# Feed-forward's first four outputs from the sum in front of its norm, with the norm's weights as two more columns

## What is computed

```python
x = layer_norm(alpha * x + mix, ln1_g[l], ln1_b[l])
ff = swiglu_ffn(x, w_ffn_gate[l], w_ffn_up[l], w_ffn_down[l])
x = layer_norm(alpha * x + ff, ln2_g[l], ln2_b[l])
...
def swiglu_ffn(x, w_gate, w_up, w_down):
    return (jax.nn.silu(x @ w_gate) * (x @ w_up)) @ w_down
```

## Time and profile before

| | |
|---|---|
| median of 3 runs | 893.04 us (893.03 to 893.29) |
| profiled execution | 894.56 us, its span 892.8 us |
| TensorE matmuls busy | 872.5 us (98%) |
| VectorE busy | 627.1 us (70%) |
| ScalarE busy | 440.3 us (49%) |
| granted TensorE clock, mean | 0.996 |

### The profile page before, as it was taken

How to read it: one execution, slowest core, us unless ns; L and a number is a source line. 1 busy time by engine, 2 the same in 40 slices (tenths; PEclk the granted TensorE clock), 3 DMA queues, 4 the chain that set the end, 5 groups by cost and what they waited for, 6 DMA issues and landing times.

```text
span 892.8 us, 13280 instructions
## 1 busy us (share of the span) xinstructions
PE 872.5 (98%) x5324; PEld 709.2 (79%) x5324; DVE 627.1 (70%) x1252; ACT 440.3 (49%) x750; POOL 21.2 (2%) x16
## 2 busy tenths in 40 slices
PE   8999999999999999999999999999999999999996
PEld 4678477776687777877998888988999888888885
DVE  5532757594836759966699999978688775665666
ACT  3351515543723356555544444566554665555552
POOL 0000000000000000000002121100000000000000
PEclk9999999999999999999999999999999999999999
DMA  9784551100354033203556656441366365546541
GB/s 351 284 319 171 203 197 61 48 25 1 119 196 161 16 130 142 84 23 142 167 189 188 190 173 204 142 143 59 103 196 210 113 201 206 188 175 204 190 164 47
DMA packets 39997, 136.68 MB, mean 153 GB/s; under 512 B 4352, under 2 KB 4480, under 8 KB 39680
## 3 DMA queue, kind: packets, MB, share of 16 engines
q1 hardware_dynamic: 38928, 130.48, 42.8%
q10 hardware_dynamic: 1008, 5.36, 1.6%
HBM read 134.77 MB, written 1.05 MB: 152 GB/s over the span
## 4 chain that ended last, share of the span: by engine, by line
PE 68%; DVE 25%; ACT 3%; DMA 2%; issue 1%; SPq 0%; DVEq 0%; ACTq 0%
PE ps L414 8%; DVE wlo L1472 7%; PE ps L971 6%; DVE AF L1941 6%; PE ps L415 4%; PE ps L369 4%; PE ps L370 4%; PE ps L374 3%; PE ps L733 3%; PE ps L489 3%; PE ps L386 2%; DMA AF<-wmod 2%; PE ps L397 2%; PE ps L756 2%; PE ps L398 2%; PE ps L401 2%
## 5 line engine op out<-in xcount | busy, mean ns | idle before, releaser
L1472 DVE TENSOR_TENSOR wlo<-raw,whi 128x1024 fp32r<-128x1024 f32 (+2 forms) x204 | 231.6, 1158 | 34.4 <-ACT whi L1009 34.2
L1009 ACT ACTIVATE whi<-raw 128x1024 fp32r<-128x1024 f32 (+2 forms) x204 | 203.5, 1005 | 86.2 <-DMA raw<-wpack 45.8
L369 PE MATMUL ps<-hx,whi 128*128 128x256 f32 (+1 forms) x384 | 115.4, 300 | 0.3 <-ACT AF L1350 0.3
L414 PE MATMUL ps<-hx,whi 128*128 128x512 f32 x320 | 113.9, 398 | 0.0
L370 PE MATMUL ps<-hx,whi 128*128 128x256 f32 (+1 forms) x384 | 112.0, 292 | 0.0
L374 PE MATMUL ps<-hx,wlo 128*128 128x256 f32 (+1 forms) x332 | 96.9, 292 | 0.0
L415 PE MATMUL ps<-hx,wlo 128*128 128x256 f32 x320 | 89.8, 281 | 0.0
L369 PEld LDWEIGHTS ps<-hx,whi 128*128 128x128 f32 x384 | 73.3, 191 | 3.8 <-issue 2.3
L370 PEld LDWEIGHTS ps<-hx,whi 128*128 128x128 f32 x384 | 73.4, 191 | 2.0 <-issue 0.7
L459 PE MATMUL ps<-whi,hx 128*128 128x512 f32 (+1 forms) x192 | 71.7, 373 | 0.2 <-ACT acc L1078 0.2
L414 PEld LDWEIGHTS ps<-hx,whi 128*128 128x128 f32 x320 | 60.1, 188 | 14.6
(11 more groups left out here) (293 smaller groups left out, 1667.2 us busy)
## 6 DMA issues: line engine op xcount, KB each, us to landing
raw<-wpack SPq DMA_DIRECT2D x178, 512.0 KB, 4.1
AF<-wmod SPq DMA_DIRECT2D x48, 512.0 KB, 6.0
raw<-wpack SPq DMA_DIRECT2D x24, 256.0 KB, 2.7
XT<-xin SPq DMA_DIRECT2D x4, 512.0 KB, 6.0
raw<-wpack SPq DMA_DIRECT2D x4, 432.0 KB, 4.9
uq<-wuq ACTq DMA_DIRECT2D x2, 768.0 KB, 5.4
cst<-cpack ACTq DMA_DIRECT2D x1, 1093.0 KB, 8.0
AF<-wukv ACTq DMA_DIRECT2D x2, 512.0 KB, 6.7
```

The costliest lines, as they stand in the source:

```text
L369: e.matmul(o, wh[:, b], xh(k), start=j == 0, stop=False, skip_group_check=True)
L414: e.matmul(ps.ap(key, 512).rearrange("p (s n) -> p s n", s=2), wh[:, b], K.hx[:, :, k, 0:256], start=k == 0, stop=False, skip_group_check= ...
L1009: e.activation(W.hi(i), W.raw(i), ACT.Copy).then_inc(*HI.up(j))
L1472: e.tensor_tensor(W.lo(i), W.raw(i), W.hi(i), ALU.subtract).then_inc(*LO.up(j))
```

## The change

Four things, all around the first norm of the second block.

1. fg0, up0, fg1 and up1 are made by a new function `lin_raw` from the sum in front of the norm, scaled by the norm's weight g. Rows of 258 columns are multiplied: 256 tokens, then two columns with the norm's weight and bias. So each output has, beside the product, the product of the weight with g and with b, from which mean, scale and bias are put in afterwards (`normed`, three instructions on DVE for each of the four outputs, with PSUM read by two of them, and a bias in the silu). The rows lie in the second half of `hx`, whose row grows from 512 to 528 columns. ACT makes the high half of each scaled tile (`raw_high`), DVE the low half (`raw_low`), tiles 0 to 4 during the `w_o` stage and 5 to 7 after the inverse root.
2. The sums and the two spreads of the norm are issued by PE between the first three k of `lin_raw`; the `keep` matmuls there go away. ACT copies m and r from PSUM to SBUF, and DVE reads them there.
3. The transposes and their copies move from f = 0 to 3 to f = 2 to 5. fg2 and up2 are put in the banks of s1 and s2, fg3 and up3 in those of m and r.
4. The conversions are placed anew: fg2 in front of the norm's tiles, up2's high half on ACT at tile 5 and its low half on DVE behind tile 7, fg3 at the start of f = 0, up3 at the start of f = 1.

```diff
+RAW = 2
...
@@ -403,9 +405,9 @@
         W.given[c] = M.now()
         ps.drop(key)
 
-    def lin_wide(key, wname, cols, xw):
-
-        free = ps.take(key)
+    def lin_wide(key, wname, cols, xw, at=None):
+
+        free = ps.take(key, at=at)
         c, wh, wl = weights(key, (wname, 0, tuple(range(KD)), cols), KD * P)
         pe.wait_ge(*free)
         for k in range(KD):
@@ -947,14 +949,34 @@
         pe.wait_ge(V["ln1", "dg", what], *ps.take(("ln1", what)))
         e.matmul(ps.ap(("ln1", what), 256), C("ones"), K.rs[:, z:z + 256], start=True, stop=True, skip_group_check=True).then_inc(*M.up(("ln1", what)))
 
-    keep(1)
-    ln1_sums("s1", K.acc[:, 0:256], K.XT[:, 7, XC], V["x1sum", 6], V["x1", 7])
-    ln1_sums("s2", K.acc[:, 256:512], K.sq[:, 768:1024], V["sqadd", 6], A["x1sq", 7])
-    ln1_spread("m", 256)
-    keep(2)
-    ln1_spread("r", 0)
-    keep(2)
+    rh, rl, rw = (lambda k: K.rx[:, 0, k, :]), (lambda k: K.rx[:, 1, k, :]), (lambda k: V["xr", k])
     xt3 = lambda k: V["x3", k]
+
+    def lin_raw(specs):
+
+        got = []
+        for key, wname, cols in specs:
+            free = ps.take(key)
+            got.append((weights(key, (wname, 0, tuple(range(KD)), cols), KD * P), free))
+        for k in range(KD):
+            b = slice(k * P, (k + 1) * P)
+            pe.wait_ge(A["gb"], A["xr", k], V["gb"], V["xr", k])
+            for (key, wname, cols), ((c, wh, wl), free) in zip(specs, got):
+                o = ps.ap(key, 258)
+                pe.wait_ge(*free)
+                e.matmul(o, wh[:, b], rh(k), start=k == 0, stop=False, skip_group_check=True)
+                e.matmul(o, wl[:, b], rh(k), start=False, stop=False, skip_group_check=True)
+                i = e.matmul(o, wh[:, b], rl(k), start=False, stop=k == KD - 1, skip_group_check=True)
+                if k == KD - 1:
+                    i.then_inc(*M.up(key))
+                    W.given[c] = M.now()
+            if k == 0:
+                ln1_sums("s1", K.acc[:, 0:256], K.XT[:, 7, XC], V["x1sum", 6], V["x1", 7])
+                ln1_sums("s2", K.acc[:, 256:512], K.sq[:, 768:1024], V["sqadd", 6], A["x1sq", 7])
+            if k == 1:
+                ln1_spread("m", 256)
+            if k == 2:
+                ln1_spread("r", 0)
 
     def down(f, ts):
 
@@ -977,12 +999,13 @@
     for f in range(KF):
         cc = (P * f, P)
         if f == 0:
-            lin_many([((nm, j), f"w_ffn_{w}_2", 0, (P * j, P), x2h, x2l, 256) for j in range(2) for nm, w in (("fg", "gate"), ("up", "up"))], lambda k: A["x3h", k], xt3)
-        elif f > 1:
-            lin_wide(("fg", f), "w_ffn_gate_2", cc, xt3)
-            lin_wide(("up", f), "w_ffn_up_2", cc, xt3)
-        if f < 4:
-            t, q = f // 2, f % 2
+            lin_raw([((nm, j), f"w_ffn_{w}_2", (P * j, P)) for j in range(2) for nm, w in (("fg", "gate"), ("up", "up"))])
+        elif f >= RAW:
+            at = [ps.bank.get(("ln1", x)) if f < RAW + 2 else None for x in (("s1", "s2") if f == RAW else ("m", "r"))]
+            lin_wide(("fg", f), "w_ffn_gate_2", cc, xt3, at[0])
+            lin_wide(("up", f), "w_ffn_up_2", cc, xt3, at[1])
+        if RAW <= f < RAW + 4:
+            t, q = (f - RAW) // 2, (f - RAW) % 2
             pe.wait_ge(A["x3", 4 * q + 3], *ps.take(("x3t", f)))
             for j in range(4):
                 i = e.transpose(ps.ap(("x3t", f), P, j * P), K.XT[:, 4 * q + j, 256 + t * P:384 + t * P], C("ident"))
@@ -1405,14 +1428,27 @@
             highs(("ao", m))
         ac.wait_ge(V["mgs", m], M["attn2"])
         e.activation(hh[:, m, 0:256], g.Gt[:, m, :], ACT.Copy, scale=0.5).then_inc(*A.up(("mg", m)))
+    def raw_high(m):
+        ac.wait_ge(V["x1", m])
+        e.activation(K.rx[:, 0, m, 0:256], XT[:, m, XC], ACT.Copy, scale=C("l1g", m, 1)).then_inc(*A.up(("xr", m)))
+
     highs(("wo", 0))
+    ac.wait_ge(K.c2["cst"], M["attn2"])
+    e.activation(K.rx[:, 0, :, 256:258], C("l1g", 0, 16).rearrange("p (s k) -> p k s", s=2), ACT.Copy).then_inc(*A.up("gb"))
     for m in range(KD):
         if m < 7:
             highs(("wo", m + 1))
+            raw_high(m)
         z = m % 4 * 256
         ac.wait_ge(V["x1", m], V["sqadd", m - 4] if m >= 5 else V["sqadd", 1] if m == 4 else None)
         e.activation(K.sq[:, z:z + 256], XT[:, m, XC], ACT.Square).then_inc(*A.up(("x1sq", m)))
+    raw_high(7)
     e.dma_start(K.AF[:, 3072:5120], K.l2rows).then_inc(*K.l2_in.up("rows"))
+    highs(("up", 1), 1)
+    for what, z in (("m", 0), ("r", 256)):
+        ac.wait_ge(M["ln1", what])
+        e.activation(K.acc[:, z:z + 256], ps.ap(("ln1", what), 256), ACT.Copy).then_inc(*A.up(("ln1", what)))
+        ps.give(("ln1", what), A.now())
 
     def x3(k):
         z = k % 4 * 256
@@ -1424,28 +1460,31 @@
         e.activation(hh[:, k, 0:256], K.sq[:, z:z + 256], ACT.Identity, bias=C("l1b", k, 1)).then_inc(*A.up(("x3h", k)))
         if k:
             x3(k - 1)
+        if k == 5:
+            highs(("up", 1), 2)
     x3(KD - 1)
-    highs(("up", 1), 1)
     for m in range(KF):
         z = m % 2 * 256
+        if m < RAW:
+            highs((("up", 1), ("fg", 2))[m], 3)
         highs(("fg", m))
         side = K.AF[:, 8192 + 2 * z:8704 + 2 * z]
         ac.wait_ge(M["fg", m], V["fu", m - 2] if m >= 2 else None)
-        if m < 2:
-            e.activation(K.AF[:, z:z + 256], ps.ap(("fg", m), 256), ACT.Silu).then_inc(*A.up(("fg", m)))
-            ps.give(("fg", m), A.now())
+        if m < RAW:
+            ac.wait_ge(V["fgn", m])
+            e.activation(K.AF[:, z:z + 256], side[:, 0:256], ACT.Silu, bias=K.modrow[:, 4 * m + 1:4 * m + 2]).then_inc(*A.up(("fg", m)))
         else:
             e.activation(side[:, 0:256], ps.ap(("fg", m), 256, 256), ACT.Copy).then_inc(*A.up(("fgs", m)))
             ac.wait_ge(V["fga", m])
             e.activation(K.AF[:, z:z + 256], side[:, 0:256], ACT.Silu).then_inc(*A.up(("fg", m)))
         highs(("up", m))
-        if m > 1:
+        if m >= RAW:
             ac.wait_ge(M["up", m])
             e.activation(side[:, 256:512], ps.ap(("up", m), 256, 256), ACT.Copy).then_inc(*A.up(("ups", m)))
-        ac.wait_ge(V["fu", m], M["fd", m - 8, 1] if m >= 8 else None)
+        ac.wait_ge(V["fu", m], M["fd", m - 8, 1] if m >= 8 else M["up", RAW - 1])
         e.activation(K.fh[:, m % 8, :], K.AF[:, 512 + z:768 + z], ACT.Copy).then_inc(*A.up(("f", m)))
-        if m < 4:
-            t, q = m // 2, m % 2
+        if RAW <= m < RAW + 4:
+            t, q = (m - RAW) // 2, (m - RAW) % 2
             ac.wait_ge(M["x3t", m])
             e.activation(g.x3t[:, t, 512 * q:512 * q + 512], ps.ap(("x3t", m)), ACT.Copy, scale=ALPHA).then_inc(*A.up(("x3t", m)))
             ps.give(("x3t", m), A.now())
@@ -2091,7 +2130,13 @@
             dv.wait_ge(A["x1sq", m - 1], V.now())
             e.tensor_tensor(K.acc[:, 256:512], K.sq[:, 0:256] if m == 2 else K.acc[:, 256:512], K.sq[:, z:z + 256], ALU.add).then_inc(*V.up(("sqadd", m - 1)))
 
+    def raw_low(m):
+        dv.wait_ge(A["xr", m])
+        e.scalar_tensor_tensor(out=K.rx[:, 1, m, 0:256], in0=XT[:, m, XC], scalar=C("l1g", m, 1), in1=K.rx[:, 0, m, 0:256], op0=ALU.mult, op1=ALU.subtract).then_inc(*V.up(("xr", m)))
+
     lows(("wo", 0), 4)
+    dv.wait_ge(A["gb"])
+    e.tensor_tensor(K.rx[:, 1, :, 256:258], C("l1g", 0, 16).rearrange("p (s k) -> p k s", s=2), K.rx[:, 0, :, 256:258], ALU.subtract).then_inc(*V.up("gb"))
     for m in range(KD):
         dv.wait_ge(M["wo", m])
         e.scalar_tensor_tensor(out=XT[:, m, XC], in0=XT[:, m, XC], scalar=ALPHA, in1=ps.ap(("wo", m), 256), op0=ALU.mult, op1=ALU.add).then_inc(*V.up(("x1", m)))
@@ -2099,6 +2144,8 @@
         x1_sums(m)
         if m < 7:
             lows(("wo", m + 1), 4)
+            if m >= 2:
+                raw_low(m - 2)
 
     v, mu, u, w, m2 = (K.nrm[:, 2 * i:2 * i + 2] for i in range(5))
     def diagonal(what, z, x):
@@ -2107,8 +2154,8 @@
                         ALU.mult).then_inc(*V.up(("ln1", "dg", what)))
 
     def x1_centre(k):
-        dv.wait_ge(M["ln1", "m"])
-        e.tensor_tensor(XT[:, k, XC], XT[:, k, XC], ps.ap(("ln1", "m"), 256), ALU.add).then_inc(*V.up(("x1c", k)))
+        dv.wait_ge(A["ln1", "m"])
+        e.tensor_tensor(XT[:, k, XC], XT[:, k, XC], K.acc[:, 0:256], ALU.add).then_inc(*V.up(("x1c", k)))
 
     dv.wait_ge(M["ln1", "s1"])
     e.tensor_scalar(mu, ps.ap(("ln1", "s1"), 2), -1.0 / D, None, ALU.mult, ALU.bypass).then_inc(*V.up())
@@ -2122,6 +2169,9 @@
     ps.give(("ln1", "s2"), V.now())
     rsqrt(v, u, w)
     diagonal("r", 0, v)
+    lows(("up", 1), 1)
+    for m in range(5, 8):
+        raw_low(m)
     for k in range(2):
         x1_centre(k)
 
@@ -2132,26 +2182,39 @@
 
     for k in range(KD):
         z = k % 4 * 256
-        dv.wait_ge(M["ln1", "r"], V["x1c", k], A["x3", k - 4] if k >= 4 else None, V["x3", k - 4] if k >= 4 else None)
```

(36 more changed lines are left out.)

## The result

The median of the changed kernel is 901.13 us (899.17 to 901.52, 6 executions) against 893.18 (893.03 to 895.43, 6 executions) of the kernel before: ratio 1.0078, interval 1.0063 to 1.0092. The forecast was 896.2, range 894.6 to 898.2. The direction was right; the size was not, and the time lies 2.9 us above the range.

What follows compares the result with a forecast made beforehand. PE was taken to bound the kernel, except for a 6.37 us hole at the norm. Gain 3.64 less stalls 6.99 is 3.35 slower, 3.14 by another reading; 3.2 taken: 893.04 + 3.2 = 896.2 us, range 894.6 to 898.2.

Steps and rivals of the forecast that it cites:

- `lin_raw` and the gain of 3.64: At the norm, lin_raw's 96 matmuls start at 691.53 and end at 705.85, not 709.49: 3.64 us gained on PE.
- DVE up to the normed tiles: DVE's chain behind the norm's sums: first scaling at 699.87, 3.14 us later than before, last normed tile ready at 709.20.
- The stalls: PE waits before fg2, up2, up3 and both halves of down(0): 0.98, 0.79, 0.63, 2.43 and 2.16, together 6.99 us.
- net of 3.35 and 3.14: Loss on PE: 3.35 us slower from stalls less gain, 3.14 us slower by comparing down(0)'s end with the old profile.
- likeliest case: Whole kernel: a loss of 2 to 4.6 us, chance 0.75.
- Faster: Rival: DVE and ACT meet fd0's deadlines, only the fg2 and up2 stalls remain; 1.9 us faster, 891.1; chance 0.05.
- about the same: Rival: the DVE and ACT chain is some 2 us shorter than counted, giving 894.2 us; chance 0.10.
- The clock: Rival: two PE pauses at down(0) drop the clock to 1.2 GHz, 2.75 to 5.6 us more, 899 to 902; chance 0.07.
- reading of the tail: After PE's last matmul at 883.85 the clock was still 1.00 at 888 to 889, so a pause over 4 us seemed harmless.
- The sign that the forecast named: The forecast would be wrong if the clock fell below 1.00 in PE's stretch between 705 and 728.
- 258 columns are dear: Rival: lin_raw's 258-column matmuls cost as much as 512 (0.235 us), about 7 us longer, 900; chance 0.03.
- The base: Starting time of the sum: the old kernel's median of 893.04 us, leaving out the profiled execution's 1.5 us above it.

Runs made afterwards that it cites:

- version with rows of 516: Changed kernel with sooner ACT conversions, less DVE work before down(0), three DVE conversions moved behind it, hx rows of 516 columns: 894.66 us, ratio 1.0009.
- other banks: Changed kernel with transposes and their copies at f = 4 to 7 and down(0)'s outputs in the banks of fg0, up0, fg2, up1: 900.87 us, ratio 1.0075.

## Why the prediction was wrong

The 8.1 us between 893.04 and 901.13 hold 5.2 in the back part: 195.37 - 192.32 = 3.05 without the fall of the clock, and 2.15 of the fall. The other 2.9 lie in the front part, and they are two things: the wider rows, and an early dip that only one side has. 893.04 is the time of an execution without the dip; four of the six of the changed kernel took 900.96 to 901.52 at a mean clock of 0.993 to 0.994, which fits fall and dip together. Like against like the front part's share is smaller: with no dip on either side 899.48 or 899.17 stand against 893.04, 6.1 to 6.4 us, and with the dip on both 901.61 stands against 894.57, 7.0. Less 5.2, the wider rows have 0.9 to 1.8 us there, and the dip, which isn't the change's doing, the rest of the 2.9.

- **`lin_raw` and the gain of 3.64.** Right: 14.28 us for 14.32. The price of 0.121 us for 258 columns held.
- **DVE up to the normed tiles.** Right to 0.1 us.
- **The stalls.** Start times right to 0.15 us at each of the five places, and the net of 3.35 and 3.14 came out as 3.05 (without the fall). In part that is luck: it holds 0.7 us that the wider rows give back in the feed-forward; against the same rows without the change it is 195.37 - 191.64 = 3.73, 0.4 to 0.6 more than reckoned. The likeliest case of the forecast is therefore what happened, as far as it went. "Faster" and "about the same" needed a chain 2 to 4 us shorter; it wasn't.
- **The clock.** This is the step that failed: *"so a pause of over 4 us left it at 2.4 GHz ... The rows speak against it for pauses of this length"*, and the 0.07 that came of it: the sum of the forecast has no term for the clock at all, and the fall took 1.9 to 2.2 us. The reading of the tail was right for that one execution and chance as evidence. How long the clock stays at 1.00 behind the last matmul differs from profile to profile: over 4.0 us in nine of the twenty, 2.1 to 4.0 in the others. One of these (the version with rows of 516), PE's last pair and the stretches with the granted clock:

```profile
884.14 0.62 PE L993 MATMUL ps<-whi,hx 128*128 128x512 f32 x2
...
884.00:886.00 2.00, 0.76 (x4) 0.28 (x2) 2.00 (x4) 0.00 (x0) 0.00 (x0) 1.00 0.45 175
886.00:888.00 2.00, 0.00 (x0) 0.00 (x0) 1.86 (x7) 1.24 (x2) 0.00 (x0) 0.70 0.24 91
```

The chip showed the fall in two of three profiles of the changed kernel (not in the one with rows of 544), in "other banks" and, in a pause of 1.57 us, in the kernel without its zeros; with zeros in the pauses, never in three. The sign that the forecast named, a clock below 1.00 in that stretch, came. The price given for the rival, 899 to 902 us, held the median, but by luck: its cost of 2.75 to 5.6 us was too high, and the fall alone doesn't explain the miss, for with zeros in the pauses and no fall the time is still 900.15 and 900.24, above the range. And the kernel itself had the hint: three groups of zeros in the norm, of which the nearest pauses left were 0.79 and 0.34 us. The Trainium skill ("TensorE: Matmul & The Clock Gate", Part 1 on the clock gate) calls the throttled state the default and says that activity releases it; it adds that the monitor runs free of the kernel, so that the place of a change varies from run to run. The traces agree with the second: the fall comes 1.35 us into the first half of `down(0)` in one execution, 0.8 us into it in another and not at all in a third, with a pause of 2.2 to 2.3 us ahead of it each time. With the first the falls at the pauses agree; the early dip, where the profile counts PE as busy, doesn't follow from it as it stands.

- **The wider rows.** A second failed step: a term that the sum didn't have at all. The forecast doesn't name the row of 528 among the costs; by itself it costs 0.9 to 1.6 us net over the whole kernel, some 2 in a part of it that the change doesn't touch.
- **258 columns are dear.** Rightly given little.
- **The base.** The 1.5 us of the profiled execution that the forecast left out are the early dip. Leaving them out made the base too low: 893.04 is the middle of three executions without it, while the kernel before beside the experiments has medians of 893.88 to 894.61 (11 to 29 executions each), and most executions of either kernel have the dip.

Not settled: what brings the early dip, why the fall at 724 comes in some executions only, whether the second pause has any part in it, and by what a row step other than 512 makes most of these matmuls longer and L414 shorter.

## What to carry to other kernels

A pause has a second price beside its own length: behind or in pauses of 1.6 to 2.3 us TensorE's clock fell here, in some executions or in all, and cost about 2 us more. One profile in which a longer pause did no harm doesn't rule that out. A handful of zero matmuls in the pauses cost nothing here, so a change that opens pauses should fill them. A deadline that PE meets today with 6 us to spare is spent by reordering: add up on DVE and ACT every instruction that lands in front of it. A buffer whose rows are made wider is a change to every matmul that reads it, wherever it stands in the kernel. And where executions differ by a dip of 1.9 us, a forecast and its result are compared only with the dip on both sides or on neither.

## What the hardware showed unexpectedly

- The clock fell to 1.2 GHz inside a pause of 1.57 us (behind matmuls of one column); behind pauses of 2.28 and 2.23 us, while the next matmuls ran; and behind two of 2.27 and 1.90 us. With pauses of 2.26 and some 1.8 us (two profiles), and of 1.66 and 0.85 us (one), it didn't.
- After the last matmul the clock stayed at 1.00 for 2.1 to 5.3 us, over twenty profiles.
- The same program has, in some executions, a stretch of 1.2 GHz at about 84 us; it costs about 1.9 us. The profile counts PE as busy without a break there, but just ahead of it this is matmuls of one column each (24 in the timeline); such stand ahead of the fall at 695.3 too, in the kernel without its zeros. Whether these bring it wasn't tested. In the kernel before, PE's timeline, then busy by stretch just ahead of the dip and in it:

```profile
81.59 1.84 PE L610 MATMUL ps<-cst,wk 128*128 128x1 f32 x16
83.30 1.27 PE L614 MATMUL ps<-cst,acc 128*128 128x1 f32 x8
...
82.00:83.90 1.90, 1.90 (x19) 1.90 (x19) 0.00 (x0) 0.00 (x0) 0.00 (x0) 1.00 0.00 0
84.00:87.20 3.20, 3.20 (x14) 3.20 (x15) 1.41 (x9) 0.00 (x0) 0.00 (x0) 0.50 0.00 0
```

- A row step of 528 in place of 512 columns makes a matmul with its stationary tile from that buffer 398 ns long in place of 393 (L459), one that streams 512 columns of a row 395 in place of 390 (L388), and one that streams 256 columns of each of two rows 393 in place of 398 (L414). No other step tried (516, 520, 536, 544) looked free in the front part.
